# One queue for all weights: the modulation rows 32 to 175 go from GpSimd's program into SyncE's

## The reference, cut to what matters

```python
def hybrid_layer(x, c_act, g, w_ada, b_ada, w_in, w_out, dec_f, dec_b):
    mod = c_act @ w_ada + b_ada                    # 2048 x 6144
    shift, scale, gate = jnp.split(mod, 3, axis=-1)
    h = rms_norm(x, g) * (1.0 + scale[:, None]) + shift[:, None]
    proj = jnp.einsum('bsd,df->bsf', h, w_in)
    ...
    return x + gate[:, None] * out

def second_block(...):
    c_act = jax.nn.silu(c)
    for l in range(DEPTH_2):                       # 2
        mod = c_act @ w_mod[l] + b_mod[l]          # 2048 x 6144 each
        shift, scale, gate = jnp.split(mod, 3, axis=-1)
        h = x * (1.0 + scale[:, None]) + shift[:, None]
        ...                                        # shared_kv: c_act @ w_mod_kv, 2048 x 4096
        x = layer_norm(DN_ALPHA * x + gate[:, None] * y, ln_g[l], ln_b[l])
```

## Time and profile before

| | |
|---|---|
| time, median of 3 runs | 1424.46 us (1424.04 to 1425.03) |
| the profiled execution, its own time | 1424.35 us |
| span of the profile | 1422.5 us (1.85 us lie around it) |
| PE, DVE, ACT, POOL busy | 1399.1, 1187.4, 709.2, 123.2 us |
| moved by DMA | 451.00 MB, mean 317 GB/s |
| of it SP's queue q1, POOL's queue q0 | 281.06 MB, 152.09 MB |

### The profile page before, as it was taken

One profiled execution on the slowest core, in us unless ns is written; L12 is line 12 of the kernel. 1 busy time (PEld: TensorE's weight loads), 2 busy tenths in 40 slices (PEclk: granted clock), 3 DMA queues, 4 the chain that ended last, 5 costly groups with the idle time before them and its releaser, 6 DMA issues.

```text
span 1422.5 us, 19860 instructions
## 1 busy us (share of the span) xinstructions
PE 1399.1 (98%) x6926; PEld 1172.6 (82%) x6926; DVE 1187.4 (83%) x1547; ACT 709.2 (50%) x1051; POOL 123.2 (9%) x203
## 2 busy tenths in 40 slices
PE   6999999999999999999999999999999999999997
PEld 4888788888888888888888888888888888888886
DVE  5999999888998789898778789978898877677566
ACT  5655435654445644444456553474345645465440
POOL 0000010113100000110011101000010012110000
PEclk9999999999999999999999999999999999999999
DMA  9999999988996899999977799689799788775762
GB/s 368 417 415 417 414 413 404 348 303 302 410 414 206 314 338 384 399 382 372 342 226 256 238 333 364 246 285 375 271 344 351 247 290 287 230 247 167 271 193 97
DMA packets 101978, 451.00 MB, mean 317 GB/s; under 512 B 11793, under 2 KB 16257, under 8 KB 78337
## 3 DMA queue, kind: packets, MB, share of 16 engines
q1 hardware_dynamic: 73296, 281.06, 54.4%
q0 software_dynamic: 21008, 152.09, 27.7%
q10 hardware_dynamic: 7586, 16.69, 3.1%
HBM read 447.63 MB, written 2.15 MB: 316 GB/s over the span
## 4 chain that ended last, share of the span: by engine, by line
PE 91%; DMA 3%; DVE 3%; issue 1%; ACT 1%; POOL 0%; ACTq 0%; SPq 0%; DVEq 0%
PE bank L941 16%; PE bank L943 16%; PE bank L924 16%; PE bank L942 16%; PE bank L922 8%; PE bank L876 3%; PE bank L878 3%; PE bank L877 3%; DMA raw<-in_t_steps 2%; PE bank L1180 2%; PE bank L1138 2%; DVE gw L1776 1%; PE bank L920 1%; DMA squares<-in_c 1%; PE bank L1156 1%
## 5 line engine op out<-in xcount | busy, mean ns | idle before, releaser
L1264 ACT CAST w_hi<-raw 128x1024 fp32r<-128x1024 f32 x434 | 455.2, 1051 | 604.6 <-PE bank L943 309.0
L1748 DVE TENSOR_TENSOR w_lo<-raw,w_hi 128x1024 fp32r<-128x1024 f32 x360 | 438.0, 1224 | 170.6 <-ACT w_hi L1264 167.7
L1776 DVE CUSTOM_DVE_ANT_0 gw<-gw,c_act 128x2048 f32<-128x2048 f32 x176 | 401.8, 2285 | 1.6 <-DMA gw<-in_t_ada 1.5
L942 PE MATMUL bank<-w_lo,act_parts 128*128 128x512 f32 x1008 | 392.4, 389 | 0.0
L941 PE MATMUL bank<-w_hi,act_parts 128*128 128x512 f32 x952 | 382.6, 402 | 0.5 <-issue 0.2
L943 PE MATMUL bank<-w_hi,act_parts 128*128 128x512 f32 x952 | 371.6, 390 | 0.0
L924 PE MATMUL bank<-act_parts,w_hi 128*128 128x512 f32 x960 | 338.0, 394 | 0.0
L922 PE MATMUL bank<-act_parts,w_lo 128*128 128x256 f32 x1024 | 276.7, 280 | 0.0
L942 PEld LDWEIGHTS bank<-w_lo,act_parts 128*128 128x128 f32 x1008 | 189.6, 188 | 37.6
L924 PEld LDWEIGHTS bank<-act_parts,w_hi 128*128 128x128 f32 x960 | 180.1, 188 | 39.0
L943 PEld LDWEIGHTS bank<-w_hi,act_parts 128*128 128x128 f32 x952 | 178.6, 188 | 38.4
(11 more groups left out here) (215 smaller groups left out, 1081.8 us busy)
## 6 DMA issues: line engine op xcount, KB each, us to landing
raw<-in_t_steps SPq DMA_DIRECT2D x464, 512.0 KB, 6.7
gw<-in_t_mod POOLq DMA_DIRECT2D x96, 1024.0 KB, 8.2
gw<-in_t_ada SPq DMA_DIRECT2D x32, 1024.0 KB, 9.3
gw<-in_t_kv_mod POOLq DMA_DIRECT2D x32, 1024.0 KB, 8.4
gw<-in_t_ada POOLq DMA_DIRECT2D x16, 1024.0 KB, 8.8
area<-gate_rows ACTq DMA_DIRECT2D x3, 1024.0 KB, 10.5
bias<-forget_sums ACTq DMA_DIRECT2D x16, 192.0 KB, 6.5
area<-in_ln_g ACTq DMA_DIRECT2D x2, 1024.0 KB, 7.9
```

Source lines behind the costliest of these rows:

```text
L942: nc.tensor.matmul(dst, hi, w_lo[:, j % SLOTS, k], start=False, stop=False)
L1264: nc.scalar.copy(w_hi[:, b], raw[:, j % SLOTS]).then_inc(hi_ready, 1)
L1748: nc.vector.tensor_tensor(w_lo[:, j % SLOTS], raw[:, j % SLOTS], w_hi[:, j % LEAD].bitcast(F32), ALU.subtract).then_inc(lo_ready, 1)
L1776: nc.vector.tensor_tensor_reduce(out=w, in0=w, in1=c_act[:].rearrange("p (t n) -> p t n", t=TT), scale=1.0, scalar=0.0, op0=ALU.mult, op1= ...
```

## The change

SP takes over the 144 rows. Behind which load a row stands follows from the table that sets the gemvs: row g + 3 stands behind load k when gemv g stands in step k - 8. Rows 32, 33 and 34, the first, have a place of their own (`FIRST_ROWS`). SP waits for gemv g before it issues the row, and its next load stands behind that wait. SP's loop is written out, since rows stand at irregular places. POOL's `load` loses the DMA and its wait and is called `follow`; the wait for a load in pairs 8 and 18 goes too. Two sets of semaphores for the landing of rows become one.

```diff
+FIRST_ROWS = {32: 50, 33: 53, 34: 53}
...
+def rows_behind(k):
+
+    if k < FIRST_PAIR * PAIR_STEPS + 2:
+        return [g for g in range(2, HEAD_TILES) if ROW_BEHIND[g] == k]
+    late = [g for g in range(2, HEAD_TILES) if ROW_BEHIND[g] == k]
+    late += [g for g, at in FIRST_ROWS.items() if at == k]
+    pair, h = divmod(k - SLOTS, PAIR_STEPS)
+    return late + [g + GEMV_RING for at, g in gemv_steps(pair) if h <= at < h + 1 and g + GEMV_RING < MODS * KT]
...
                 load_step(k * P, k)
-                for g in range(2, HEAD_TILES):
-                    if ROW_BEHIND[g] == k:
-                        load_row(g)
+                for g in rows_behind(k):
+                    load_row(g)
...
-            with sp.Fori(0, WEIGHT_CHUNKS) as i:
-                for j in range(STEPS):
-                    k = FRONT_STEPS + j
-                    sp.wait_ge(half_used, i * STEPS + (k - SLOTS + 1))
-                    load_step(i * (STEPS * P) + k * P, j)
+            for k in range(FRONT_STEPS, FRONT_STEPS + WEIGHT_CHUNKS * STEPS):
+                sp.wait_ge(half_used, k - SLOTS + 1)
+                load_step(k * P, k)
+                for g in rows_behind(k):
+                    load_row(g)
...
-            def load(g):
-                dst, landed, _ = gemv_slot(g)
-                if g >= GEMV_RING:
-                    pool.wait_ge(gemv_used, g - GEMV_RING + 1)
+            def follow(g):
...
-                src, row = MOD_SRC[b]
-                pool.dma_start(dst, src[row + k * P:row + (k + 1) * P].rearrange("p (t n) -> p t n", t=TT)
-                               ).then_inc(landed, 16)
...
                                 inverse_root(("norm", NORM_PAIR.index(pair), 0))
-                                pool.wait_ge(raw_landed[LEAD - 1], 16 * (2 * pair + 3))
-                            load(g + GEMV_RING)
+                            follow(g + GEMV_RING)
```

More of the change, by code:

```diff
@@ L445, in two_blocks @@
         raw_landed = [sem(f"raw_landed{i}") for i in range(SLOTS)]
-        front_landed = [sem(f"front_landed{i}") for i in range(GEMV_RING)]
-        gw_landed = [sem(f"gw_landed{i}") for i in range(GEMV_RING)]
+        row_in = [sem(f"row_in{i}") for i in range(GEMV_RING)]
         rows_landed = sem("rows_landed")
@@ L589, in gemv_slot @@
             row = gw[:, i].rearrange("p (t n) -> p t n", t=TT)
-            if g < HEAD_TILES:
-                return row, front_landed[i], 16 * (g // GEMV_RING + 1)
-            return row, gw_landed[i], 16 * ((g - HEAD_TILES) // GEMV_RING + 1)
+            return row, row_in[i], 16 * (g // GEMV_RING + 1)
         def mod_at(g):
@@ L809, in _ @@
             for g in range(HEAD_TILES, HEAD_TILES + GEMV_RING):
-                load(g)
+                follow(g)
             for p in range(FIRST_PAIR, PAIRS):
```

## The result

The changed kernel takes 1434.0 us (median of 4 runs, 1433.14 to 1435.3) against 1424.39 us, a ratio of 1.0069 with an interval of 1.0057 to 1.0081: slower by 9.6 us, where no change that can be told was forecast. Its profiled execution took 1433.14 us, with a span of 1431.3.

A forecast was written before the change was run, and what follows sets the result against it. PE was taken as the bound, busy 98% of the span with 2.2 us idle from 150 to 1400 us. The terms summed as 1424.35 + 0.3 - 0.3 = 1424.35 us (1424.4 against the median), range 1422.8 to 1427.5.

The forecast's parts named there:

- first rival: From 150 to 200 us, loads standing behind a whole row on one queue stall PE: 1433 us, chance 0.13.
- second rival: In the full stretch, SP's waits for gemvs run the DMA queue dry and lose bandwidth: 1428.4 us, chance 0.05.
- third rival: In pairs 8 and 18, rows ahead of loads delay DVE's norm chain and so PE: 2.4 us, 1426.8 us, chance 0.08.
- signs named: Profile marks: if right, some 165 SP waits, POOL busy some 45 us; if wrong, under 400 GB/s in 150 to 200 us.
- the holds: SP keeping a released load behind a gemv wait, at most 6.9 us after 150 us, 3.8 us to spare: cost 0.
- Rows 2 to 31: Argument from rows already on SP's queue: SP waited 73.2 us for gemvs there and PE did not stop.
- The price for load 54: Two rows now ahead of this load; landing at 169.4 us, split up to 0.6 us later: +0.3 us (0 to +0.6).
- The norm pairs: Pairs 8 and 18: three rows each ahead of loads, reaching PE with 1.2 us at most per pair; taken as 0.
- POOL without rows: Pair 6: without row DMAs, POOL's roots take 0.7 us and DVE regains 2.1 us: -0.3 us (0 to -0.33).
- The loop: SP's program written out without a loop: loads lose a few register instructions, hidden in SP's waits; 0.
- the order behind load 54: For later loads, rows and loads swap places by up to one row (2.53 us) and the queue keeps up: 0.

## Why the prediction was wrong

The number of the first rival, 1433, came out, but that is luck: not by its mechanism and not in its place. The second rival, loss by holds, was nearest to the mechanism, put at 0.05 and at +4 us, and the third had the norms right. Of the signs named, those of the change itself came (166 waits of SP, POOL busy 44.9 us), and so did those of being wrong: 384 GB/s in 150 to 200 us, and 8.9 us of PE's idle time where 0 to 5 were allowed.

- **The step that failed is the holds, at 0.** The prediction took one hold, the longest it found (6.9 us), and set it against one load on an empty queue (15.3 of 19.1 us) or on a queue of median depth. It did not follow a run of holds, and it let a full queue hide the hold: "a held load therefore lands at about its old time". Load 117 landed 9.9 us later. Where rows stand one to a load and DVE is the slow one, SP is tied to DVE's pace, and each hold eats up spare that the next load needs; the engines meanwhile stay nearly full (share 0.98 in 350 to 385 us), and the time in the queue comes on top: 7.7 us of hold, 10.8 to land, a cast of 1.05 and a split of 1.22 are 20.8 us, where a load had 19.1. In 350 to 430 us this run moved 381 GB/s instead of 413, over 80 us 2.6 MB or 6.2 us of transfer; about 2.2 us of it (an estimate: 385 GB/s for 411 over 35 us) were lost ahead of 385 us, when load 117 had landed, and the rest is in part a consequence of its lateness. Waits alone: +8.1 us; rows without waits: -1.5.
- **The place was chosen by one stretch.** 150 to 200 us was taken as the tightest; the earlier trace rows had 350 to 380 us with DVE at 29.97 of 30 and the DMA share at 1.01, read only for the roots. The loss in 150 to 260 us was 1.1 us, in pair 7 2.9 us of standing and, by the clock of 0.83 over 10 us, some 1.7 of the 2.7 us of slower matmuls (an estimate).
- **Rows 2 to 31 were no evidence.** SP's 73.2 us of waits there did no harm under a table of their own; what made them harmless was not asked, and no run here tells.
- **The price for load 54 held.** Taken at +0.3 (0 to 0.6): the load, issued at 160.5, landed after 8.5 us, at 169.0 (169.4 foreseen), its split began 0.2 us later than before, and PE stands 0.39 us ahead of the step at 182.89 us, 0.34 more in 150 to 200 us.
- **The norm pairs, at 0 with 1.2 us each as the bound**, cost 2.0 and 0.9 us. This is the third rival, 2.4 us for both, at 0.08, and here the order on the queue does count: by waits alone the norms lose nothing, and with the six rows off SP's queue nothing either. DVE's 1.33 us of waiting for PE in pair 8 are gone, and PE waits 1.23 us for the split of a late load and 0.81 us behind the norm. With all rows one load later pair 8 still loses 1.2 us (48.52 busy in 430 to 480). The bound left out the lag from pair 7, without which pair 8 loses 0.4 us.
- **The clock was not in the sum.** PE's matmuls were slower behind the stall of 2.85 us, and its busy time rose by 2.7 us in all.
- **POOL without rows** was put at -0.3 by roots at 0.7 us. In the changed kernel POOL has no rows, and three roots of pair 6 take

```profile
330.34 0.69 POOL L772 TENSOR_TENSOR rstd<-mean_sq,minus_half 128x2 f32<-128x2 f32 x1
...
336.55 2.62 POOL L772 TENSOR_TENSOR rstd<-mean_sq,minus_half 128x2 f32<-128x2 f32 x1
...
343.57 1.53 POOL L772 TENSOR_TENSOR rstd<-mean_sq,minus_half 128x2 f32<-128x2 f32 x1
```

so the 2.64 us of the earlier trace rows need no row's DMA, DVE's wait for the roots is 1.4 us (under 0.5 foreseen), and the agreement that the prediction saw with the Trainium skill (DMA: Bandwidth & Descriptors, section SWDGE vs HWDGE vs iDMA) was one of neighbours only. What makes a root slow stays open.
- **The loop, and the order behind load 54,** both at 0, were right outside the norm pairs: a program written out costs nothing, and with every row ahead of loads, but hardly a load held, the kernel is no slower.

## What to carry to other kernels

A wait in an engine's program is a wait for everything that stands behind it. When a DMA with its own condition moves into another queue's program, list what that wait holds, for how long, and whether holds follow one another; on full DMA engines the time in the queue comes on top of the hold. Then place the DMA where its condition is already met. Here one place later in the order was worth 11 us. The kernel with the rows placed by the trace (1422.3 us, ratio 0.9988) and the one with the rows two loads later (0.9987) are the fastest; the runs don't tell them apart.

## What was not expected of the hardware

POOL's drain at the end of the program took 8.02 us in the kernel before, 2.06 in kernels whose POOL issues no rows, and 10.38 in one where it issues 22 fewer than before; where SP ends first, the kernel waits for it. Why fewer rows gave the longer drain is open. PE's clock fell to 0.83 over 10 us behind stalls of 2.85 and 2.39 us, and not behind one of 2.50; with the rows one load earlier it stayed at 1.00 behind one of 2.64 us and fell to 0.83 behind one of 2.54. So a short stall may or may not be paid twice.
